# Head norms with tokens in rows, and a new order for the third block up to the output product

## What is computed

```python
h = rms_norm_2(x, norm_mix_g); z = h @ w_in
u, v, q, kv, gl = jnp.split(z, splits, axis=-1)
a = spatial_gating_unit(gelu(u), gelu(v), ...)      # layer norm of v, 8 groups of 128x128 causal weights
# b: gated sum of three branches, 8 query heads on 2 key heads of width 64
q = rms_norm_2(q.reshape(B, T, H, G, 64), q_norm_g)             # head norms
kc = rms_norm_2(compress_blocks(k_cmp, ...), k_norm_g[0]); vc = compress_blocks(v_cmp, ...)
k_slc = rms_norm_2(k_slc, k_norm_g[1]); k_win = rms_norm_2(k_win, k_norm_g[2])
b = g[0] * compressed_attention + g[1] * selected_attention + g[2] * window_attention
mixed = concatenate([rms_norm_2(a, g0), rms_norm_2(b, g1)]); x = x + mixed @ w_out
# memory attention: 4 heads of width 128
mq = rms_norm_2((rms_norm_2(x) @ w_mq).reshape(B, T, 4, 128), q_g)   # head norms
mk, mv = split(rms_norm_2(mem) @ w_mkv); mk = rms_norm_2(mk.reshape(B, M, 4, 128), k_g)
x = x + softmax(mq @ mk * 128 ** -0.5) @ mv @ w_mo
x = x + relu(rms_norm_2(x) @ w_ff1)**2 @ w_ff2
```

## Time and profile before

| | us |
|---|---|
| median of 3 runs (1338.57 to 1342.06) | 1339.59 |
| the profiled execution | 1340.14 |
| its span in the profile | 1338.3 |
| third block, first pair of slabs to first product of slab 19 | some 883 to 1079.5 |
| from there to the end of memory attention (first product of slab 25) | 1079.5 to 1143.8 |

### The profile page before, as it was taken

One profiled execution on the slowest core, in us unless ns is written; L12 is line 12 of the kernel. 1 busy time (PEld: TensorE's weight loads), 2 busy tenths in 40 slices (PEclk: granted clock), 3 DMA queues, 4 the chain that ended last, 5 costly groups with the idle time before them and its releaser, 6 DMA issues.

```text
span 1338.3 us, 23540 instructions
## 1 busy us (share of the span) xinstructions
PE 1283.6 (96%) x10293; PEld 1240.2 (93%) x10293; DVE 835.8 (62%) x923; ACT 670.4 (50%) x948; POOL 90.3 (7%) x65
## 2 busy tenths in 40 slices
PE   3999999999999999999999999999999998999998
PEld 2999999989999999999889999998798887999998
DVE  5478547567654559745657774468658767667542
ACT  4466545456534447645545553445346445455432
POOL 3000010110001100002010000112000100100000
PEclk7999999999999999999999999999698999999999
DMA  5734554336655354444344656655421222467552
GB/s 180 244 101 137 177 161 146 104 125 194 217 190 189 115 158 131 158 135 149 126 127 147 199 190 204 197 146 168 129 95 64 95 95 64 126 190 220 189 190 95
DMA packets 195572, 202.91 MB, mean 152 GB/s; under 512 B 5716, under 2 KB 191847, under 8 KB 195471
## 3 DMA queue, kind: packets, MB, share of 16 engines
q1 hardware_dynamic: 192704, 194.82, 45.7%
q0 software_dynamic: 2464, 5.99, 1.6%
q10 hardware_dynamic: 303, 0.61, 0.2%
HBM read 200.33 MB, written 3.16 MB: 152 GB/s over the span
## 4 chain that ended last, share of the span: by engine, by line
PE 79%; DVE 8%; ACT 5%; DMA 5%; issue 2%; POOL 1%; SPq 0%; DVEq 0%; ACTq 0%
PE bank L560 13%; PE bank L561 13%; PE bank L562 13%; PE bank L2245 7%; PE bank L2243 7%; PE bank L2241 7%; DVE w_lo L524 3%; ACT w_hi L514 2%; PE bank L603 2%; PE bank L605 2%; PE bank L611 2%; PE bank L2158 2%; DMA raw<-in_w_in_dram 1%; PE bank L2142 1%; PE bank L2084 1%
## 5 line engine op out<-in xcount | busy, mean ns | idle before, releaser
L524 DVE TENSOR_TENSOR w_lo<-raw,w_hi 128x2048 fp32r<-128x2048 f32 (+7 forms) x210 | 424.2, 2029 | 342.5 <-ACT w_hi L514 342.2
L514 ACT ACTIVATE w_hi<-raw 128x2048 fp32r<-128x2048 f32 (+7 forms) x210 | 355.4, 1704 | 364.5 <-PE bank L2245 133.7
L560 PE MATMUL bank<-act_hi,w_hi 128*128 128x256 f32 x1096 | 307.3, 280 | 0.0
L561 PE MATMUL bank<-act_lo,w_hi 128*128 128x256 f32 x1096 | 304.6, 278 | 0.0
L562 PE MATMUL bank<-act_hi,w_lo 128*128 128x256 f32 x1096 | 304.6, 278 | 0.0
L2241 PE MATMUL bank<-h_hi,w_hi 128*128 128x256 f32 x768 | 212.5, 277 | 0.0
L2245 PE MATMUL bank<-h_hi,w_lo 128*128 128x256 f32 x768 | 212.3, 276 | 0.0
L2243 PE MATMUL bank<-h_lo,w_hi 128*128 128x256 f32 x768 | 212.3, 276 | 0.0
L560 PEld LDWEIGHTS bank<-act_hi,w_hi 128*128 128x128 f32 x1096 | 206.8, 189 | 0.8 <-issue 0.3
L561 PEld LDWEIGHTS bank<-act_lo,w_hi 128*128 128x128 f32 x1096 | 207.1, 189 | 0.2
L562 PEld LDWEIGHTS bank<-act_hi,w_lo 128*128 128x128 f32 x1096 | 206.7, 189 | 0.0
(11 more groups left out here) (358 smaller groups left out, 2167.7 us busy)
## 6 DMA issues: line engine op xcount, KB each, us to landing
raw<-in_w_up_dram SPq DMA_DIRECT2D x32, 1024.0 KB, 5.4
raw<-in_w_down_dram SPq DMA_DIRECT2D x32, 1024.0 KB, 5.1
raw<-in_w_ff_dram SPq DMA_DIRECT2D x32, 1024.0 KB, 5.5
raw<-in_w_in_dram SPq DMA_DIRECT2D x23, 1024.0 KB, 5.5
raw<-in_w_xk_dram SPq DMA_DIRECT2D x8, 1024.0 KB, 5.1
raw<-in_w_xv_dram SPq DMA_DIRECT2D x8, 1024.0 KB, 5.2
raw<-in_w_mix_out_dram SPq DMA_DIRECT2D x8, 1024.0 KB, 5.2
raw<-in_w_xq_dram SPq DMA_DIRECT2D x8, 1024.0 KB, 5.2
```

Of the source, the lines that this page charges most:

```text
L514: ins = act.activation(d, r, ACT.Copy)
L524: ins = dve.tensor_tensor(d, r, h.bitcast(F32), ALU.subtract)
L560: pe.matmul(o, stat_hi, mov_hi, start=first, stop=False)
L561: pe.matmul(o, stat_hi, mov_lo, start=False, stop=False)
```

## The change

Head norms 0 to 2 and 4 to 7 (3 stays as it was) sum with tokens in rows: four fp32 matmuls (eight instructions) whose stationary operand is a 128-column slice of head_sq and whose moving operand is two columns of the block matrix (one column of ones for n of 4 and more), so that the sums of 128 tokens lie on 128 partitions, 8 or 4 columns in all. head_root takes the root of these into head_inv. A new DVE step head_inverse inverts 128x8 or 128x4 and copies it, broadcast, over head_sq 128x512. A new TensorE step `hb` (head_spread, four fp32 matmuls against the identity, eight instructions) brings it back into the same bank with channels on the partitions, and head_norms multiplies from the bank. The bank is released by the norm, not by the root.

The order of all three engines is new up to slab 19; fillers are cut from 73 counts to 22. ACT takes three evacuations from DVE (two of memory keys, cturn). The lists of ACT and DVE follow TensorE's order: attentions 0 to 5 run between slabs 7 and 13, compressed scores on either side of slab 13, memory turns ahead of slab 14, memory keys' norms near slabs 16 to 18. The table loads of ACT that were implied are in part explicit.

```diff
-WARM_2 = {("pair", 0): ("y0", 4), ("hs", 1): ("hs1", 2), ("cht", 0): ("cht0", 3), ("slab", 9): ("gates", 10), ("slab", 10): ("kc", 4),
-          ("hs", 3): ("hs3", 3), ("slab", 11): ("g0", 2), ("pv", 1): ("g2", 3), ("scores", 8): ("scores8", 6),
-          ("mem", 2): ("mem2", 2), ("ot", 2): ("ot2", 10), ("slab", 19): ("w0", 2), ("hs", 6): ("hs6", 6),
-          ("scores", 12): ("scores12", 14), ("slab", 25): ("mo0", 2)}
+WARM_2 = {("pair", 0): ("y0", 4), ("ot", 2): ("ot2", 2), ("slab", 19): ("w0", 2), ("hs", 6): ("hs6", 6), ("hb", 6): ("scores12", 2),
+          ("scores", 12): ("scores12", 4), ("slab", 25): ("mo0", 2)}
 TE_ORDER_2 = (
-    [("pair", 0), ("stat", 0), ("slab", 2), ("slab", 3), ("slab", 4), ("hs", 0), ("sgw", 0), ("sgw", 1),
-     ("slab", 5), ("slab", 6), ("hs", 1), ("hs", 2), ("slab", 7), ("cht", 0), ("slab", 8), ("slab", 9), ("cht", 1),
-     ("slab", 10), ("hs", 3)]
-    + [("scores", u) for u in range(4)] + [("slab", 11), ("slab", 12), ("turn", 0), ("scores", 4), ("turn", 1),
-     ("pv", 0), ("scores", 5), ("turn", 2), ("pv", 1), ("slab", 13), ("turn", 3), ("pv", 2), ("turn", 4), ("pv", 3),
-     ("slab", 14), ("turn", 5), ("pv", 4), ("pv", 5)]
-    + [("vturn", 0), ("cscores", 0), ("cscores", 1)] + [("mem", b) for b in range(4)]
-    + [("scores", u) for u in range(6, 10)] + [("slab", 15), ("sgu", 0), ("sgu", 1), ("slab", 16), ("hs", 4), ("hs", 5),
-     ("cturn", 0), ("cpv", 0), ("cpv", 1), ("turn", 6), ("scores", 10), ("turn", 7), ("pv", 6), ("scores", 11),
-     ("turn", 8), ("pv", 7), ("slab", 17), ("turn", 9), ("pv", 8), ("turn", 10), ("pv", 9), ("turn", 11), ("pv", 10),
-     ("pv", 11), ("slab", 18)] + [("ot", b) for b in range(4)]
-    + [("slab", s) for s in range(19, 23)] + [("pair", 23), ("stat", 1), ("hs", 6), ("hs", 7)]
+    [("pair", 0), ("stat", 0), ("slab", 2), ("slab", 3), ("slab", 4), ("hs", 0), ("hs", 1), ("sgw", 0), ("sgw", 1),
+     ("slab", 5), ("hb", 0), ("hb", 1), ("hs", 2), ("slab", 6), ("hb", 2), ("cht", 0), ("slab", 7),
+     ("scores", 0), ("scores", 1), ("slab", 8), ("scores", 2), ("cht", 1), ("scores", 3), ("slab", 9), ("turn", 0), ("turn", 1),
+     ("slab", 10), ("scores", 4), ("pv", 0), ("scores", 5), ("pv", 1), ("turn", 2), ("turn", 3), ("slab", 11),
+     ("pv", 2), ("pv", 3), ("turn", 4), ("turn", 5), ("hs", 3), ("slab", 12), ("pv", 4), ("pv", 5), ("scores", 6),
+     ("scores", 7), ("vturn", 0), ("cscores", 0), ("slab", 13), ("cscores", 1), ("scores", 8), ("scores", 9), ("turn", 6)]
+    + [("mem", b) for b in range(4)] + [("slab", 14), ("scores", 10), ("turn", 7), ("pv", 6), ("pv", 7), ("cturn", 0),
+     ("slab", 15), ("cpv", 0), ("cpv", 1), ("scores", 11), ("turn", 8), ("turn", 9), ("slab", 16), ("hs", 4), ("pv", 8),
+     ("pv", 9), ("turn", 10), ("turn", 11), ("sgu", 0), ("sgu", 1), ("hb", 4), ("hs", 5), ("slab", 17), ("pv", 10),
+     ("pv", 11), ("hb", 5), ("slab", 18)] + [("ot", b) for b in range(4)]
+    + [("slab", s) for s in range(19, 23)] + [("pair", 23), ("stat", 1), ("hs", 6), ("hs", 7), ("hb", 6), ("hb", 7)]
...
-            signal = {"stat": "root", "sgw": "sgw_evac", "hs": "hs_root", "vturn": "vblk", "cht": "ch_evac",
+            signal = {"stat": "root", "sgw": "sgw_evac", "hs": "hs_done", "vturn": "vblk", "cht": "ch_evac",
...
                 if n >= 2:
-                    act.wait_ge(once["hs_done"], n - 1)
+                    act.wait_ge(once["hs_spread"], {2: 1, 3: 2, 4: 3, 5: 2, 6: 4, 7: 5}[n])
+                if n == 5:
+                    act.wait_ge(once["hs_done"], 4)
...
-            def head_norms(n, targets, width):
-
-                r = head_sq[:, n % 2, 0:width]
+            def head_inverse(n):
+
                 dve.wait_ge(once["hs_root"], n + 1)
-                dve.reciprocal(r, r).then_inc(once["hs_rstd"], 1)
-                dve.wait_ge(once["hs_rstd"], n + 1)
...
+                w = 8 if n < 4 else 4
+                r = head_inv[n % 2][:, 0:w]
+                then_next(dve.reciprocal(r, r))
+                dve.tensor_copy(head_sq[:, n % 2, :].rearrange("p (w c) -> p w c", w=w),
+                                r.unsqueeze(2).broadcast_to([P, w, 512 // w])).then_inc(once["hs_rstd"], 1)
+
+            def head_norms(n, targets):
...
+                    r = bank(f"hs{n}", DEPTH)
+                    dve.wait_ge(once["hs_spread"], n + 1 - (n > 3))
...
-                w = 30 if n == 3 else 512
-                over = cst[:, C_BLOCK:C_BLOCK + P] if n < 4 else ones[:, :]
-                pe.matmul(b[:, 0:w], over, head_sq[:, n % 2, 0:w], start=True, stop=True).then_inc(once["hs_mm"], 1)
...
+                over = cst[:, C_BLOCK:C_BLOCK + P:64] if n < 4 else ones[:, 0:1]
+                w = over.shape[1]
+                for j in range(4):
+                    ins = pe.matmul(b[:, w * j:w * j + w], head_sq[:, n % 2, P * j:P * j + P], over, start=True, stop=True)
+                ins.then_inc(once["hs_mm"], 1)
+
+            def head_spread(n):
+
+                b = bank(f"hs{n}", DEPTH)
+                pe.wait_ge(once["hs_rstd"], n + 1)
+                for j in range(4):
+                    ins = pe.matmul(b[:, P * j:P * j + P], head_sq[:, n % 2, P * j:P * j + P], ident, start=True, stop=True)
+                ins.then_inc(once["hs_spread"], 1)
```

Of DVE's new list, the stretch that the steps below speak of most:

```diff
             split_lo(dve, DEPTH, 7)
+            head_norms(1, [(q_t[:, 0:2, :], q_t[:, 0:2, :], N_Q, 0, 512)])
+            head_inverse(2)
...
+            bias_and_max(DEPTH, 11)
+            turned_out(DEPTH, 8)
+            attention_out(2)
             split_lo(dve, DEPTH, 18)
+            turned_out(DEPTH, 10)
+            head_inverse(4)
...
-            split_lo(dve, DEPTH, 20)
+            split_lo(dve, DEPTH, 19)
             attention_out(3)
...
             over_norms(0)
+            head_inverse(5)
+            split_lo(dve, DEPTH, 20)
+            over_norms(1)
+            memory_key_norms(1)
             split_lo(dve, DEPTH, 21)
-            over_norms(1)
             for b in range(4):
                 o_rest(DEPTH, b, 4 * (b // 2), b % 2)
-            memory_key_norms(1)
```

More of the change, by code:

```diff
@@ L1208, in _ @@
                 .then_inc(once["ln_root"], 1)
[L1209 to L1214, removed]
+            load_table(ACT.Exp)
             act.wait_ge(sig["slab_used"], v2("slab_used", 15))
@@ L1240, in _ @@
                 if n == 0:
-                    turned_out(DEPTH, 11)
-                    act.wait_ge(once["sgu_out"], TI)
-                    ab_squares(0)
-                    ab_squares(1)
-                    ab_root(0)
+                    split_hi(act, DEPTH, 20)
+                    for i in range(TI):
+                        act.wait_ge(once["b_sum"], TI + i + 1)
+                        ab_squares(2 + i)
+                    ab_root(1)
             split_hi(act, DEPTH, 21)
-            for n in range(TI):
-                act.wait_ge(once["b_sum"], TI + n + 1)
-                ab_squares(2 + n)
-            ab_root(1)
             for b in range(4):
@@ L1827, in _ @@
-            then_next(dve.reciprocal(flat_gates, flat_gates))
-            turned_out(DEPTH, 0)
-            split_lo(dve, DEPTH, 14)
-            bias_and_max(DEPTH, 4)
-            gelu_poly(0)
-            bias_and_max(DEPTH, 5)
-            turned_out(DEPTH, 2)
-            split_lo(dve, DEPTH, 15)
-            gelu_poly(1)
-            attention_out(0)
-            turned_out(DEPTH, 4)
-            gelu_out(0)
-            gelu_out(1)
-            split_lo(dve, DEPTH, 16)
             dve.wait_ge(once["ch_lo"], 2)
@@ L1861, in _ @@
-            gelu_out(2)
-            gelu_out(3)
+            gelu_poly(0)
+            turned_out(DEPTH, 4)
+            split_lo(dve, DEPTH, 14)
+            gelu_out(0)
+            head_inverse(3)
+            head_norms(3, [(kc[:, :, 0:N_CMP], kc_raw.rearrange("p (v n) -> p v n", v=2), N_K, 0, 30)])
+            gelu_poly(1)
+            attention_out(1)
+            bias_and_max(DEPTH, 6)
+            bias_and_max(DEPTH, 7)
+            gelu_out(1)
             dve.wait_ge(once["vturned"], 1)
@@ L1869, in _, with compressed_softmax @@
             ins.then_inc(once["vblk"], 1)
-            for v in range(2):
+            def compressed_softmax(v):
                 p3 = c_p[:, v].rearrange("p (a n) -> p a n", n=32)
@@ L1883, in _ @@
                     .then_inc(once["c_ready"], 1)
+            compressed_softmax(0)
+            split_lo(dve, DEPTH, 15)
+            dve.wait_ge(once["g_out"], 2)
+            then_next(dve.tensor_reduce(ln_stat[:, 0:2], v_dil[:, :, :], AX.X, ALU.add))
+            then_next(dve.tensor_scalar(ln_stat[:, 0:2], ln_stat[:, 0:2], -1.0 / 512, None, ALU.mult))
+            dve.tensor_tensor(v_dil[:, :, :], v_dil[:, :, :], ln_stat[:, 0:2].unsqueeze(2).broadcast_to([P, TI, 512]),
+                              ALU.add).then_inc(once["ln_center"], 1)
+            gelu_poly(2)
+            compressed_softmax(1)
+            bias_and_max(DEPTH, 8)
+            bias_and_max(DEPTH, 9)
+            turned_out(DEPTH, 6)
```

(14 more changed lines are left out.)

215 lines of the change are left out of this document (117 added, 98 removed).

## The result

The change makes the kernel faster, but by less than half of what was forecast. Over 17 executions each the median goes from 1340.55 to 1332.72 us; the ratio is 0.9948 with a 95% interval from 0.9934 to 0.9962, which is 7.0 us (5.1 to 8.8) of 1340. Forecast was 1323, a gain of 16.8. The time lies inside the range that was given, near its upper end; the size of the gain is wrong. The profiled execution of the changed kernel took 1331.32, 8.8 less than the one of before (1340.14), so its trace can be held against the sum term by term. Of all executions timed for this text one, of the kernel before with its fillers cut, took 3410.64 us and is left out of its ratio.

What follows compares the result with a forecast made beforehand. TensorE, busy 96% of the span, was taken as the bound, with DVE before the clock fell. Gains of 14.4 us up to slab 19 and 2.4 at memory queries, 16.8 in all, gave 1323; range 1306 to 1335.

Steps and rivals of the forecast that it cites:

- What bounded the kernel before: Third block, 919 to 1080: TensorE busy 150.55 of 161 us, partly fillers and half speed; DVE's reciprocals before the clock fell.
- Head norms: Five norms before slab 19: DVE gains 12 us; TensorE's sums and spreads, at 0.11 an instruction, add 3.6.
- Waits of the new order: TensorE waits at hb 2 (3.2), pv 7 (1.5), slab 16 (2.1) and hb 5 (3.7): together 10.5 us, none to 20.
- pv 7: Wait for turned probabilities that leave ACT behind eight memory evacuations: 1.5 us, between 0 and 3.0.
- TensorE's work: From slab 4's end, at full clock: 114.7 us with new sums and spreads; 112.9 to slab 18's end without waits.
- The tail: Slab 18's end to slab 19: memory values' evacuation, split_hi 21, split_lo 21, four o_rest; 7.4 us in place of 8.9.
- Half clock: From inside slab 9 to slab 11, +11.0 us; two spells of 3.4 behind the compressed scores, +3.4.
- Ten fillers become two; they hid nothing but the clock: Tail ahead of slab 19: fillers cut at no cost, slab 19 starting at 1050.7 with a full clock throughout.
- Memory queries: Norms 6 and 7, on the chain: 8.19 us become about 5.0, gain 3.2, taken as 2.4.
- The lower bound of 0.7: Memory queries' gain in us at half clock, to which the one-column sums might lead.
- waits take the place of the fillers: DVE's list late by as much again as in the four waits, +10.5: 1333.5; chance 0.17 for 1329 to 1335.6.

Runs made afterwards that it cites:

- the version with all that helped: Changed kernel with four waits moved away by order, slab 9 moving 256 columns, and fillers in the stands left: 1305.67 us, ratio 0.9752 to the kernel before.

## Why the prediction was wrong, by its own steps

- **What bounded the kernel before** was half right. The reciprocals did bound the first stretch: with the new norms alone in the old order, slab 11 comes 5.1 us sooner in the trace. But the half clock over slab 9 cost the old order nothing: with it taken from there, slab 10 started no sooner. The forecast counted 12.6 us of surplus in the whole 0.50 stretch and took it out of the old time; for slab 9's part it was right to do so only because the new order also removes the wait that the surplus lay beside.
- **Head norms**: right. Sums at 0.115 an instruction for the 0.11 taken, copies at 0.43 to 0.46 for the 0.6 taken. The Trainium skill ("TensorE: Matmul & The Clock Gate", "Wait — 56ns, not 53.3ns?") had a floor of some 25 ns for small moving sizes; with two columns the trace shows 0.115 us, so the row decides here as it did for slab 9.
- **Waits of the new order**: right in place and in sum, 11.3 for 10.5. pv 7 alone was 1.3 too short; it came near its upper bound of 3.0.
- **TensorE's work**: right. The forecast's 112.9 plus the measured waits (11.3) and half of the busy time in the spells up to slab 18 (20.4, by the windows above) is 144.6; slab 18 ended at 1062.1, 144.1 behind slab 4's end.
- **The tail**: right, 7.4 from slab 18's end to slab 19 (the four pieces of the forecast add up to 7.3).
- **Half clock**: this is the term that failed. Slab 9's spell was right: 11.9 for the 11.0 taken. For everything else the forecast took 3.4, for the compressed scores. In this execution these brought no spell (in the profiled ones of five versions of it they are followed by one or two of 3.4), but the four waits, priced at their length alone, each did: 1.7 + 3.3 + 1.7 + 1.7 = 8.4, 5.0 more. With 0.9 more at slab 9, 0.8 more of waits and 0.5 less work, slab 19 came some 6.3 later than forecast.
- **"Ten fillers become two; they hid nothing but the clock"**: the sentence was right and its price was left out. Their cut cost 2.3 us in slabs 19 to 22 in this execution (26.7 in place of 24.4), which fillers alone gave back at that place.
- **Memory queries**: 2.4 forecast, 0.6 measured (39.2 us from pair 23's first product to slab 25's, 39.9 before). The lower bound of 0.7 was for half clock there, but laid to the one-column sums; the spell of 3.4 us stands behind the wait ahead of hs 6. In the version with all that helped, which has the same sums, 9 fillers in that wait and no spell, the stretch takes 37.2, a gain of 2.7. The 0.7 does not follow from the forecast's own terms either: TensorE's 0.9, 1.8 and 0.45 at half speed would take up nearly all of the 3.2.

Of the 16.8 forecast, then, 6.3 went before slab 19, 2.3 in slabs 19 to 22 and 1.8 in the memory attention, which leaves 6.4; the profiled execution gained 6.8 from the third block's first product on.

The mistake has one root. The forecast listed four stands and priced each at its length, and in another paragraph it counted spells at half clock as if they came from narrow matmuls alone. That the clock may fall in waits it did say, but left it to the range and gave it no term in the sum. It even named the rule that joins the two. The Trainium skill ("TensorE: Matmul & The Clock Gate", "HAM oscillation — how this bites in real kernels") lays the falling clock to stretches in which TensorE idles. The forecast weighed this rule only at slab 9, where the trace speaks against it; at its own four stands and ahead of slab 19 the trace of the changed kernel agrees with it, five spells of 3.4 to 6.8 us. A spell does not follow every stand: the version with hb 5 moved has two without one. Both causes are shown by experiment: 256 columns take slab 9's spell away with all stands in place, and fillers take the other spells away with slab 9 unchanged. Spells right behind the compressed scores are seen in five traces; that the scores are their cause, no experiment shows. The rival "waits take the place of the fillers" was the nearest (1329 to 1335.6, chance 0.17), but its mechanism, waits twice as long, was not what happened.

What stays open: why slab 9's spell lasted 23.9 us in the changed kernel and 17.1 with the fillers or with the waits moved, through the same steps (with the fillers the clock fell 4.1 us behind slab 9's first product in place of 1.2, and rose 0.7 behind slab 11's in place of 2.2); and why executions of one kernel differ by as much as they do (1328.6 to 1337.1 for the changed kernel). Each kernel's spells were seen in one profiled execution only, but the mean granted clock is known for all: of the changed kernel's 17, the seven at 0.973 or less took 1333.0 to 1337.1, the ten above it 1328.6 to 1335.3.

## What to carry to other kernels

Price a wait of TensorE at its length plus the half of what may run behind it at the lower clock (here mostly 3.4 to 6.8 us, in a few cases none), and before cutting a filler ask whether the stand that it fills is gone; if it is not, the filler was no waste. Where matmuls with few moving columns bring the clock down, moving more columns into unused room of the bank costs little as long as the start-to-start time hardly grows (0.108 us with 24 columns; with 256, slab 9's 48 matmuls took 5.8 us up to the start of the next step, 0.12 each, 0.6 more in all). A stretch at half clock ahead of a step that waits for another engine may cost nothing, as slab 9 did in the old order: look for what the step behind it waits for before counting its surplus as gain.

## What was not expected of the hardware

A wider operand was cheaper than a narrow one: the same 48 matmuls of slab 9 took 9.55 us with 24 columns, most of it at a granted clock of 0.50, and with 256 columns ran at 1.00 throughout, for 11.5 us less of the kernel's time. And TensorE with more instructions finished sooner: 1003 in 140.9 us with fillers, against 952 in 150 without.
